# One front phase in place of modulation and projection, and the second modulation as row sums on VectorE in a hybrid RWKV-7 / mLSTM / PEER layer

## The reference

```
mod = silu(c) @ ada_w + ada_b               # 6 x 1024: sh1, sc1, gt1, sh2, sc2, gt2
mod_ctx = silu(c_ctx) @ ada_w + ada_b       # of this only sh1 and sc1 are used
h     = rmsnorm(x,   norm1_g) * (1 + sc1)     + sh1
h_ctx = rmsnorm(ctx, norm1_g) * (1 + sc1_ctx) + sh1_ctx
P = h @ w_in                                # RWKV and mLSTM features, gates
rw, qk = centred_conv3(...)                 # width 3: previous, current, next
y_a = rwkv_branch(rw)                       # context first, then latents
y_b = mlstm_branch(qk, mv, i, f, o)
x = x + gt1 * (merge(y_a, y_b, gates) @ w_out)
x = x + gt2 * peer_ffn(rmsnorm(x, norm2_g) * (1 + sc2) + sh2)
```

## Time and profile before

| | us |
|---|---|
| median of 3 runs (2966.55 to 2972.36) | 2971.43 |
| the profiled execution's own time | 2979.59 |
| its span | 2977.3 |

### The profile page before, as it was taken

The page is one execution under the profiler, slowest core; times in us unless marked ns, Lnnn a source line. Parts: engine busy times, 40 slices in busy tenths (PEclk is TensorE's granted clock), DMA queues, the critical chain, the costliest instruction groups (busy, mean ns, idle before and its releaser), DMA issues. The chain is left out here.

```text
span 2977.3 us, 53770 instructions
## 1 busy us (share of the span) xinstructions
PE 2653.2 (89%) x19972; PEld 2145.4 (72%) x19972; DVE 1251.0 (42%) x2585; ACT 1030.5 (35%) x1766; POOL 768.8 (26%) x635
## 2 busy tenths in 40 slices
PE   5698858888878599779959999997999999999998
PEld 2585427727778378568848888886888888888886
DVE  0225335544434523249974444440004444444443
ACT  2322252332223322233226666662223222222222
POOL 0420003203333034245545555552440000000000
PEclk9899968989999799989979999998999999999999
DMA  4211020120000222142224445545445555555552
GB/s 166 86 63 44 5 92 2 61 90 4 4 4 4 89 85 95 46 145 98 86 96 163 166 164 207 180 164 208 148 145 187 189 189 190 196 197 197 189 190 73
DMA packets 159610, 350.04 MB, mean 118 GB/s; under 512 B 13368, under 2 KB 79416, under 8 KB 156160
## 3 DMA queue, kind: packets, MB, share of 16 engines
q1 hardware_dynamic: 159488, 348.23, 33.4%
HBM read 276.89 MB, written 71.30 MB: 117 GB/s over the span
## 5 line engine op out<-in xcount | busy, mean ns | idle before, releaser
L85 PE MATMUL ps_a<-h_hi,u_hi 128*128 128x512 f32 x1024 | 407.5, 398 | 23.2 <-PEq L105 16.6
L86 PE MATMUL ps_a<-h_hi,u_lo 128*128 128x512 f32 x1024 | 401.2, 392 | 0.0
L87 PE MATMUL ps_a<-h_lo,u_hi 128*128 128x512 f32 x1024 | 401.1, 392 | 0.0
L2484 DVE TENSOR_TENSOR v_lo<-v_raw,v_hi 128x1024 fp32r<-128x1024 f32 x128 | 158.3, 1236 | 565.5 <-ACT v_hi L2442 565.5
L85 PE MATMUL ps_y<-gated_hi,v_hi 128*128 128x512 f32 x768 | 299.4, 390 | 3.1 <-DVE gated_lo L2486 3.1
L2442 ACT ACTIVATE v_hi<-v_raw 128x1024 fp32r<-128x1024 f32 x128 | 135.8, 1061 | 477.9 <-PE ps_a L87 469.6
L86 PE MATMUL ps_y<-gated_hi,v_lo 128*128 128x512 f32 x768 | 299.5, 390 | 0.0
L87 PE MATMUL ps_y<-gated_lo,v_hi 128*128 128x512 f32 x768 | 299.4, 390 | 0.0
L85 PEld LDWEIGHTS ps_a<-h_hi,u_hi 128*128 128x128 f32 x1024 | 194.3, 190 | 62.3 <-issue 22.7
L87 PEld LDWEIGHTS ps_a<-h_lo,u_hi 128*128 128x128 f32 x1024 | 193.7, 189 | 40.6
L86 PEld LDWEIGHTS ps_a<-h_hi,u_lo 128*128 128x128 f32 x1024 | 194.3, 190 | 38.1
(11 more groups left out here) (490 smaller groups left out, 5400.6 us busy)
## 6 DMA issues: line engine op xcount, KB each, us to landing
u_raw<-in_uT SPq DMA_DIRECT2D x128, 512.0 KB, 3.5
v_raw<-in_v SPq DMA_DIRECT2D x128, 512.0 KB, 4.8
a_scratch<-act SPq DMA_DIRECT2D x128, 256.0 KB, 2.2
w_scratch<-w_block SPq DMA_DIRECT2D x8, 4096.0 KB, 12.0
w_ring<-w_scratch SPq DMA_DIRECT2D x64, 512.0 KB, 4.4
gated<-a_scratch SPq DMA_DIRECT2D x128, 256.0 KB, 4.9
mg_raw<-in_w_merge SPq DMA_DIRECT2D x36, 512.0 KB, 3.4
ada_ring_x<-in_ada_w SPq DMA_DIRECT2D x5, 2048.0 KB, 7.8
```

The lines of the kernel that those rows point to most:

```text
L85: pe.matmul(out, wh, xh, start=first, stop=False)
L86: pe.matmul(out, wl, xh, start=False, stop=False)
L87: return pe.matmul(out, wh, xl, start=False, stop=last)
L2484: v.tensor_tensor(vl[:, q], v_raw[:, q], vh[:, q], ALU.subtract).then_inc(v_lo, 1)
```

## The change

`phase_modulation` and `phase_projection` become one `phase_front` without a barrier in between. In it:

- The constant block keeps only its memsets; the constants' loads are issued in the front, and their wait stands at its end. `w_gates` is loaded there too, and `phase_values` no longer waits for it.
- SyncE's order is written out: the first modulation tile before x; the first two weight tiles, and after their split two more, ahead of the store of h.
- Squares are made in four pairs of channel tiles; VectorE adds the two of a pair, so TensorE does four matmuls for each stream instead of eight.
- Of the first modulation, tiles 0, 2 and 1 stay on TensorE. The fourth comes as rows (`ada_rows`, 128 x 1024 each): VectorE multiplies a row tile by silu(c), spread over all partitions, and sums, once for each stream (8 instructions). The spread silu is made by 16 matmuls of a broadcast column with the identity.
- Per j the high part is now made from the scaled value by ScalarE (Identity with the shift as bias), the low part by one VectorE instruction for each stream (value plus shift minus high part), and the shifted value itself (`whole`) two channels later. GpSimd has no part in the split of h.
- Projection tiles 0 and 1 are made j by j while h is being split: `channel(0, j)` as soon as the low part of j is there, `channel(1, j - 3)` behind it. From tile 2 on the loop is as before.
- The eight later modulation tiles leave the feature phases. They come as 32 row tiles of 0.5 MB through a ring of two, for the latent stream only: `late_rows(t)` puts two row sums on VectorE behind the taps of each of tiles 0 to 15, and SyncE loads them between the weight tiles.
- `phase_rwkv_features` has no `Modulation` any more, and the class is gone.

The core of the diff:

```diff
@@ phase_front, SyncE
+            sp.dma_start(cc[:], a["cc"]).then_inc(small_in, 16)
+            sp.dma_start(b.ident[:], a["ident"]).then_inc(small_in, 16)
+            sp.dma_start(ada[0], a["ada_w"][ORDER[0]]).then_inc(ada_in[0], 16)
+            sp.dma_start(xx[:], a["xT"]).then_inc(x_in, 16)
+            sp.dma_start(xc, a["ctxT"]).then_inc(x_in, 16)
+            sp.dma_start(g1[:], a["norm1_g"]).then_inc(small_in, 16)
+            sp.dma_start(bias[:], a["ada_b"]).then_inc(small_in, 16)
+            sp.dma_start(ada[1], a["ada_w"][ORDER[1]]).then_inc(ada_in[1], 16)
...
+            for t in range(4, RW_TILES + QK_TILES):
+                sp.wait_ge(w_lo[t % 2], t // 2)
+                sp.dma_start(ring[:, t % 2], a["w_rw"][t]).then_inc(ring_in[t % 2], 16)
+                for n in range(2 * t - 6, 2 * t - 4):
+                    late_row(n)
@@ ScalarE
+            act.wait_ge(small_in, 64)
+            act.activation(th[:], cc[:], ACT.Tanh, scale=0.5).then_inc(tanh_done, 1)
...
+            for p in range(pairs):
+                if p >= 2:
+                    act.wait_ge(sum_mm, p - 1)
+                for lo, hi in halves:
+                    src = (xc if lo else xx)[:, 2 * p:2 * p + 2]
+                    m = act.activation(sq[:, p % 2, :, lo:hi], src, ACT.Square)
+                m.then_inc(sq_done, 1)
+            copy_row(0)
+            act.wait_ge(sum_mm, pairs)
...
+            def high(j):
+                act.wait_ge(scaled, 2 * j + 2)
+                for s, (lo, hi) in enumerate(halves):
+                    m = act.activation(b.hh[:, j, lo:hi], value(j)[s], ACT.Identity, bias=b.mod[:, j, s:s + 1])
+                m.then_inc(h_hi, 1)
@@ TensorE
+            for s, bank in enumerate((ps_b, ps_x)):
+                for k in range(KT):
+                    mm = pe.matmul(bank[:, k // 4, k % 4 * P:(k % 4 + 1) * P],
+                                   b.silu_c[:, k, s:s + 1].to_broadcast([P, P]), b.ident[:], start=True, stop=True)
+                mm.then_inc(bc_mm, 1)
...
+            for j in range(KT + LAG):
+                if j < KT:
+                    pe.wait_ge(h_lo, j + 1)
+                    mm = channel(0, j)
...
+                if j >= LAG:
+                    mm = channel(1, j - LAG)
@@ VectorE
+            v.wait_ge(ada_mm, 2)
+            for r in range(PER):
+                v.wait_ge(row_in[r], 16)
+                for s, silu in enumerate((silu_x[:], silu_c)):
+                    link(v.scalar_tensor_tensor(out=junk, in0=ada_rows[r].rearrange("p (a t) -> p a t", t=TC), scalar=1.0,
+                                                in1=silu.rearrange("p (a t) -> p a t", t=TC), op0=ALU.mult, op1=ALU.mult,
+                                                accum_out=raw[:, r, s:s + 1]))
...
+            def low(j):
+                v.wait_ge(h_hi, j + 1)
+                for s, (lo, hi) in enumerate(halves):
+                    m = v.scalar_tensor_tensor(out=b.hl[:, j, lo:hi], in0=h[:, j, TX:] if s else xx[:, j],
+                                               scalar=b.mod[:, j, s:s + 1], in1=b.hh[:, j, lo:hi],
+                                               op0=ALU.add, op1=ALU.subtract)
+                m.then_inc(h_lo, 1)
...
+            def late_rows(t):
+                for n in range(2 * t, min(2 * t + 2, LATE)):
+                    v.wait_ge(late_in[n % 2], (n // 2 + 1) * 16)
+                    v.scalar_tensor_tensor(out=late[:, n % 2], in0=late[:, n % 2], scalar=1.0, in1=silu_x[:], op0=ALU.mult,
+                                           op1=ALU.mult, accum_out=raw2[:, n:n + 1]).then_inc(late_done, 1)
@@ phase_rwkv_features
-            mod.copy_row(act, 0)
             act.wait_ge(norm_max, 1)
             act.activation(tmp[:], tmp[:], ACT.Ln).then_inc(norm_root, 1)
             act.wait_ge(norm_root, 1)
             act.activation(tmp[:], tmp[:], ACT.Exp, scale=-0.5).then_inc(norm_root, 1)
-            for n in range(1, n_mod):
-                mod.copy_row(act, n)
...
-            for n in range(n_mod):
-                mod.multiply(pe, n)
-            mod.turn(pe)
...
-            mod.add_bias(v)
```

More of the change, by code:

```diff
@@ L117 @@
 MOD_FIRST = 2 * D // MOD_W
-MOD_SECOND = MOD_FIRST + 3
 PER = MOD_W // P
[L122 to L161, removed]
-    def turn(self, pe):
-        pe.wait_ge(self.out, self.hi - self.lo)
-        for n in range(self.hi - self.lo):
-            for q in range(PER):
-                o = 2 * (n * PER + q)
-                mm = pe.matmul(self.ps_mod[:, o:o + 2], self.row[:, n, q * P:(q + 1) * P], self.b.ident[0:2, 0:2],
-                               start=True, stop=True)
-        mm.then_inc(self.turned, 1)
-    def add_bias(self, v):
-        lo, hi = self.lo * PER, self.hi * PER
-        v.wait_ge(self.bias_in, 16)
-        v.wait_ge(self.turned, 1)
-        v.tensor_tensor(self.b.mod[:, lo:hi, :], self.ps_mod[:, 0:2 * (hi - lo)].rearrange("p (g s) -> p g s", s=2),
-                        self.bias[:, lo:hi].unsqueeze(2).to_broadcast([P, hi - lo, 2]), ALU.add).then_inc(self.done, 1)
-        v.wait_ge(self.done, 1)
@@ L396, in _ @@
         @block.vector
         def _(v):
-            with v.Fori(0, n_r) as i:
+            link = Count(v, dve)
+            v.wait_ge(small_in, 64)
+            v.wait_ge(tanh_done, 1)
+            link(v.scalar_tensor_tensor(out=b.silu_c[:], in0=th[:], scalar=1.0, in1=cc[:], op0=ALU.add, op1=ALU.mult))
+            v.tensor_scalar(b.silu_c[:], b.silu_c[:], 0.5, None, ALU.mult).then_inc(silu_done, 1)
+            for s, (bank, to) in enumerate(((ps_b, silu_x[:]), (ps_x, silu_c))):
+                v.wait_ge(bc_mm, s + 1)
+                v.tensor_copy(to, bank[:].rearrange("p k t -> p (k t)")).then_inc(bc_out, 1)
@@ new lines, in _ @@
+            lo, hi = R_TILE * PER, (R_TILE + 1) * PER
+            v.tensor_tensor(b.mod[:, lo:hi, :], raw[:], bias[:, lo:hi].unsqueeze(2).to_broadcast([P, PER, 2]), ALU.add)
+            v.wait_ge(turned_mm, 1)
+            link(v.tensor_tensor(b.mod[:, 0:lo, :], ps_mod[:, 0:2 * lo].rearrange("p (g s) -> p g s", s=2),
+                                 bias[:, 0:lo].unsqueeze(2).to_broadcast([P, lo, 2]), ALU.add))
+            for s in range(2):
+                m = v.scalar_tensor_tensor(out=scale[:, s], in0=b.mod[:, KT:2 * KT, s], scalar=1.0, in1=g1[:],
+                                           op0=ALU.add, op1=ALU.mult)
@@ new lines, in _ @@
+            scale_by(0)
+            for j in range(KT):
+                if j + 1 < KT:
+                    scale_by(j + 1)
+                low(j)
+            def late_rows(t):
[3 more added lines that the diff above has]
+                                           op1=ALU.mult, accum_out=raw2[:, n:n + 1]).then_inc(late_done, 1)
@@ L399, in _ @@
+            for i in range(n_r):
                 for k in range(2):
```

336 lines of the change are left out of this document (182 added, 154 removed).

## The result

The changed kernel takes 2845.8 us (median of 4 runs, 2838.9 to 2851.7) against 2971.4: ratio 0.958, 95% interval 0.9552 to 0.9607. The profiled execution took 2841.6 (span 2839.3), 138.0 less than the profiled one of before.

What follows compares the result with a forecast made beforehand. Stages stand in a row with full barriers, so each touched stage's last wait counts. Gains of 30.0 (front), 3.1 (gates), 11.3 and 17.8 (features) less 0.3 make 61.9 us: 2971.4 to 2909.5, range 2896 to 2922.

Steps and rivals of the forecast that it cites:

- Its sum: Whole kernel: gains of 30.0, 3.1, 11.3 and 17.8 us less 0.3 at the projection's end make 61.9 us.
- all later stages shifted as one piece: Stages behind the touched ones: they keep their lengths and only start earlier; no size of their own.
- Start and first steps: Front: loads issued from about 1.45 us, small loads landing at 17.6 behind large ones, silu broadcast 6.1 us.
- Last modulation add: Front: the last bias add of the first modulation comes at 58 us, where it was at 68.69.
- lock rule: Front: VectorE and GpSimd share a port pair exclusively; by that rule alone the last bias add comes at 60.5 us.
- my middle way: Front: VectorE's row sums held by one GpSimd weight split, between no hold (56.8 us) and both in full (60.5).
- From there to tile 2: Projection: tile 2 starts 29.5 us after the last bias add, at 87.5 instead of 117.5, a gain of 30.0.
- Gates: Value stage: with the gates' weights loaded earlier, TensorE starts 3.1 us sooner, and all of it counts.
- Feature stages: Without the second modulation there, the context stage ends 11.3 us and the latent one 17.8 us earlier.
- Longer idleness: Before the scans TensorE idles some 22 and 32 us instead of 6; priced at nothing, at most 2 us a stage.
- the rival of the double price: VectorE's row sums run at half the rate: last bias add at 66 us, kernel 2917.5 us; chance 0.12.
- The slower rival: Projection: row and weight loads on SyncE's queue hold each other up, +112 us, kernel about 3021 us; chance 0.03.

Runs made afterwards that it cites:

- with 11 increments: The kernel before with 11 unread semaphore increments put on TensorE's queue ahead of the latent scan: 2901.4 us, ratio 0.9758 to the kernel before.
- with 34: The kernel before with 34 unread semaphore increments put on TensorE's queue ahead of the latent scan: 2903.3 us.
- with 222: The changed kernel with 222 unread semaphore increments put on TensorE's queue ahead of the latent scan: 2865.3 us.
- without the second modulation: The kernel before, feature stages' modulation left out and its columns zeroed, 150 unread semaphore increments on TensorE's queue in the projection stage: 2890.4 us.
- 190: The changed kernel with 190 unread semaphore increments put on TensorE's queue ahead of the latent scan: 2919.0 us.
- 40 increments: The changed kernel with 40 unread semaphore increments put on TensorE's queue ahead of the latent scan: 2875.8 us.

## Why the prediction was half right

**Its sum held, and the kernel gained another 71 us outside of it.** With the loop on the fast side in both, the kernel before takes 2901.4 (with 11 increments) and the changed one 2845.8, or by the two profiles' spans 2902.2 and 2839.3: 55.6 and 62.9 us, against the 61.9 of the sum. (The changed kernel's median lies between its two pairs of runs; from the faster pair it is 61.1.) The step that failed is "all later stages shifted as one piece": the forecast had no term for a stage that the diff doesn't touch. I took those stages as fixed. The latent scan isn't, and became 71.4 us shorter (314.1 to 242.7): it depends on a number that the diff does touch, TensorE's instructions ahead of it. No rival had this, and the rows gave no size for it; but the trace of before held the sign: TensorE waiting in the scan's passes for nothing but issue, at the head of each pass, and 68 of the 99 instruction packets of the run in that one stage.

**Start and first steps.** Loads from 1.52 (forecast 1.45), ScalarE's first step at 18.31 (17.6), broadcast 6.0 us (6.1). The two small loads behind the large ones set it, as forecast: the run with them in front gained 10.6.

**Last modulation add.** 60.6 where I took 58. TensorE's side was right to 0.1 us (turning done at 56.6). The term that was too small is the hold by GpSimd's two splits: two row sums of 3.24 us instead of 1.22, 4.0 in all. I had taken one split of the two. The Trainium skill's lock rule (SBUF — State Buffer, section SBUF: two separate sides) gave 60.5; it, not my middle way, agrees: two sums held by one split each. That the number fits to 0.1 us is partly luck, since the sums began 0.9 us later than I had them (46.34 for 45.4) and the hold was 4.0 instead of 4.8.

**From there to tile 2.** 25.6 us where I took 29.5. Low parts followed one another every 2.12 us, where I had 2.25 and 3.4 more in all for the copies: here it was mostly GpSimd that waited, 14.24 us for four copies that took 4.14 before, and VectorE lost only 1.5 us, in its last two instructions. The clock was low for the first 3.5 us of the projection only. The last wait before tile 2 is the split of its weights (83.76, 2.40), as forecast. The two errors, 2.6 late and 3.9 early, nearly cancel and make 31.3 of the 30.0: that this term came out so close is luck.

**Gates.** TensorE's gap fell from 7.73 to 4.75 us: 3.0 of 3.1; another 0.7 came in the stage itself.

**Feature stages.** Context 11.8 (11.3). Latent 19.2 (17.8): maximum to multiplication took 5.20 and the chain behind it 18.0, both as taken from the earlier trace rows; the rest came ahead of that: the maximum ended 31.2 us into the stage, before 32.9. Of these 1.7 us, 1.2 lie in the eight matmuls of the norm: 6.42 us before, at a mean granted clock of 0.57, and 5.20 after, at 0.71. In the kernel before with 34 and with 11 increments, which still has the modulation there, they took 5.23 and 5.37. So most of it is a difference between executions and not a gain of the change; against the run with 11 (74.9 us for the stage) the latent gain is 18.0.

**Longer idleness.** Priced at nothing to 2 us a stage. With the loop on the fast side the latent scan takes 241.1 to 243.1 us behind 31 us of idleness or more (the changed kernel, with 222, without the second modulation), and 239.6 and 240.3 behind 6 or 7: 1 to 3 us. The context scan shows none (its first pass took 34.4 us, before 35.1).

**Row sums and queue.** 1.22 us, so the rival of the double price is out. The rule of the Trainium skill behind it (Vector Engine (DVE) Microarchitecture Reference, section Points that are easy to get wrong) isn't borne out by the form with a sum either. The slower rival (rows and weights on one queue) is out by the run without them.

## What to carry to other kernels

A loop that nearly fills TensorE's instruction memory makes the time depend on how many instructions stand ahead of it: here 71 us in 2971 hung on three instructions. Before costing a change to one stage, look in the trace for a loop whose passes wait for issue and for packets on the instruction queue, and compare two versions only with such loops placed alike; otherwise a change is credited with, or blamed for, where it happens to put them. And where VectorE and GpSimd hold each other up, moving the work of one only moves the hold (3.9 us gained and 4.0 given back here), unless it goes to where nobody waits for either.

## What was not expected of the hardware

- A loop of 1730 TensorE instructions ran its passes in 29.2 us without any instruction packet, or in 39 to 41 with nine packets of 16 KB each; of the added time two thirds were idleness and one third the lower clock that followed it (0.92 for 1.00 over the pass). Between the two, a loop just over the limit was fetched in every second pass (33 us a pass).
- A semaphore increment on TensorE's queue isn't free where TensorE is waited for: 222 of them put the scan off by 30 us, 190 by 25 and 40 by 3; between these runs that is some 0.15 us each, and the first ones lie in a wait that was there anyway.
- VectorE and GpSimd hold each other up in both directions: row sums went from 1.22 to 3.24 us beside splits, and GpSimd's copies from 1.04 to 3.56 us beside scalings.
- The mLSTM stage has two lengths with the same code, 90.1 or 101.3 us. Over the stage, granted clock and busy time differ (here the changed kernel, then the one with 40 increments); the difference arises at its start:

```profile
280.90:371.00 90.10, 62.64 (x320) 36.59 (x320) 36.03 (x92) 37.51 (x132) 5.96 (x5) 0.74 0.01 4
```

```profile
282.10:383.50 101.40, 74.07 (x320) 40.79 (x320) 36.05 (x92) 37.57 (x132) 5.96 (x5) 0.64 0.01 3
```

In the first 30 us of the stage TensorE was busy equally long in both, but was granted 0.89 and did 106 matmuls in the short stage, and 0.53 and 68 in the long one (again the changed kernel, then the one with 40 increments). Why the clock rose late there stays open.

```profile
280.90:310.90 30.00, 26.07 (x106) 0.89 0.04 10
282.10:312.10 30.00, 26.21 (x68) 0.53 0.04 10
```

Open too: what fixes the border at 195, and why a loop that reaches a little into an eighth block is fetched in every second pass.
